# Norm closings in two parts of 256 tokens, in a two-block transformer forward pass

## The reference

```python
def _layer_norm(x, g, b):
    mu = jnp.mean(xf, -1, keepdims=True)
    var = jnp.mean(jnp.square(xf - mu), -1, keepdims=True)
    return (xf - mu) * lax.rsqrt(var + LN_EPS) * g + b

x = _layer_norm(ALPHA * x + h, ln1_g, ln1_b)             # twice a layer, 4 in all
x = _layer_norm(ALPHA * x + _sq_relu_mlp(x, w1, w2), ln2_g, ln2_b)
...
h = h + rms_norm(mix, ln_mix_post)                       # second block
a = rms_norm(h, ln_ffn_pre)
ff = (silu(a @ w_gate) * (a @ w_up)) @ w_down
h = h + rms_norm(ff, ln_ffn_post)
```

## Time and profile before

| | |
|---|---|
| median of 3 runs | 2173.42 us (2169.97 to 2177.93) |
| profiled execution | 2177.21 us, span 2175.4 us |
| granted PE clock, mean | 0.989 |
| PE busy | 2091.1 us, 96% |
| PEld busy | 1664.8 us, 77% |
| DVE busy | 1238.9 us, 57% |
| ACT busy | 812.7 us, 37% |
| POOL busy | 262.1 us, 12% |
| DMA | 179.24 MB, mean 82 GB/s |

### The profile page before, as it was taken

The page is one execution under the profiler, slowest core; times in us unless marked ns, Lnnn a source line. Parts: engine busy times, 40 slices in busy tenths (PEclk is TensorE's granted clock), DMA queues, the critical chain, the costliest instruction groups (busy, mean ns, idle before and its releaser), DMA issues. The chain is left out here.

```text
span 2175.4 us, 30851 instructions
## 1 busy us (share of the span) xinstructions
PE 2091.1 (96%) x12664; PEld 1664.8 (77%) x12664; DVE 1238.9 (57%) x1692; ACT 812.7 (37%) x1268; POOL 262.1 (12%) x266
## 2 busy tenths in 40 slices
PE   8999989999999999999999999999998899999996
PEld 6776867888888778888878888877666578888885
DVE  5547866642344576667563453467678638534544
ACT  4444234531332434444362322344224554222321
POOL 0000002000001000000201880020542010000002
PEclk9999999999999999999999999999999999999998
DMA  6120003222222122222122222223111042233221
GB/s 232 65 72 29 4 3 107 90 96 97 96 97 94 63 95 78 69 70 76 49 95 94 97 97 97 97 88 125 59 59 35 2 145 88 91 93 108 98 79 65
DMA packets 51676, 179.24 MB, mean 82 GB/s; under 512 B 5784, under 2 KB 5784, under 8 KB 51280
## 3 DMA queue, kind: packets, MB, share of 16 engines
q1 hardware_dynamic: 47712, 165.45, 22.9%
q10 hardware_dynamic: 3328, 8.13, 1.1%
q0 software_dynamic: 496, 3.69, 0.4%
HBM read 172.51 MB, written 4.21 MB: 81 GB/s over the span
## 5 line engine op out<-in xcount | busy, mean ns | idle before, releaser
L1150 DVE TENSOR_TENSOR w_lo<-w_raw,w_hi 128x1024 fp32r<-128x1024 f32 (+1 forms) x320 | 412.3, 1290 | 696.3 <-ACT w_hi L1143 696.0
L1248 PE MATMUL banks<-xh,w_hi 128*128 128x512 f32 x1560 | 624.6, 400 | 3.5 <-PEq L214 2.5
L1250 PE MATMUL banks<-xh,w_lo 128*128 128x512 f32 x1560 | 609.4, 391 | 0.0
L1249 PE MATMUL banks<-xl,w_hi 128*128 128x512 f32 x1560 | 609.3, 391 | 0.0
L1143 ACT ACTIVATE w_hi<-w_raw 128x1024 fp32r<-128x1024 f32 (+1 forms) x320 | 328.6, 1029 | 703.7 <-PE banks L1250 653.1
L1248 PEld LDWEIGHTS banks<-xh,w_hi 128*128 128x128 f32 x1560 | 294.1, 189 | 74.9 <-issue 13.3
L1250 PEld LDWEIGHTS banks<-xh,w_lo 128*128 128x128 f32 x1560 | 293.8, 188 | 62.8
L1249 PEld LDWEIGHTS banks<-xl,w_hi 128*128 128x128 f32 x1560 | 294.3, 189 | 58.6 <-issue 1.7
L1248 PE MATMUL banks<-hh,w_hi 128*128 128x512 f32 x688 | 269.8, 392 | 1.0 <-DVE hl L372 1.0
L1250 PE MATMUL banks<-hh,w_lo 128*128 128x512 f32 x688 | 267.7, 389 | 0.0
L1249 PE MATMUL banks<-hl,w_hi 128*128 128x512 f32 x688 | 267.7, 389 | 0.0
(11 more groups left out here) (513 smaller groups left out, 2558.2 us busy)
## 6 DMA issues: line engine op xcount, KB each, us to landing
w_raw<-in_w SPq DMA_DIRECT2D x128, 512.0 KB, 3.4
w_raw<-in_w_gu SPq DMA_DIRECT2D x44, 512.0 KB, 3.4
w_raw<-in_w_c_in SPq DMA_DIRECT2D x40, 512.0 KB, 3.4
w_raw<-in_w_ab_in SPq DMA_DIRECT2D x27, 512.0 KB, 3.5
w_raw<-in_w_in SPq DMA_DIRECT2D x25, 512.0 KB, 3.5
w_raw<-in_w_down SPq DMA_DIRECT2D x16, 384.0 KB, 3.1
w_raw<-in_w_down SPq DMA_DIRECT2D x16, 320.0 KB, 2.8
w_raw<-in_w_ab_out SPq DMA_DIRECT2D x8, 512.0 KB, 3.4
```

Source lines behind the costliest of these rows:

```text
L1150: dve.tensor_tensor(lo[:, 0:n], core.raw[u % RAW][:, 0:n], hi[:, 0:n].bitcast(F32), ALU.subtract).then_inc(core.split_ready, 1)
L1248: pe.matmul(bank, hi[:, w], src.xh[:, kk, :], start=kk == 0, stop=False)
L1249: pe.matmul(bank, hi[:, w], src.xl[:, kk, :], start=False, stop=False)
L1250: mm = pe.matmul(bank, lo[:, w], src.xh[:, kk, :], start=False, stop=last)
```

## The change

The 512 tokens are taken as two halves of 256 (HALVES) around each norm. In short:

- **Last block** (in_halves): the last block of a product with a norm has two PSUM banks. All tiles of its last unit are swept for the first half (256 columns), `half` is signalled, then for the second half. Between the tiles of the second sweep PE does the mean matmuls of the first half and begins those of the second (pe_half). If the block has two units, the first one's tiles are done half after half.
- **Closing** (act_last, dve_last, in place of act_tail, dve_tail): both engines do the first half's closing during the second sweep, then wait for unit_used and do the second half's.
- **Next product** (by_items, in place of outer behind a norm): tiles 0 to 2 are made and used as six half items, first half first, then tiles 3 to 7 whole. The mean matmuls that close the second half come after the first item (pe_second). The banks of three units are accumulated over column halves.
- **Squares and spill** of tiles 0 to 2 (norms 4, 5) wait until both halves are there.
- **Final norm**: tiles 0 to 4 in halves, 13 items; VectorE does all additions; stores go item by item, in turn from SP and ScalarE.
- The dummy matmuls behind norms are gone. A product with a norm takes one bank more, so the ring of banks turns one further.

The diff, cut to its core:

```diff
+HALVES = (slice(0, T // 2), slice(T // 2, T))
+IN_HALVES = 3
+FINAL_IN_HALVES = 5
+def in_items(n):
+    return [(k, cols) for cols in HALVES for k in range(n)] + [(k, slice(0, T)) for k in range(n, KD)]
 class LayerNorm:
-    def pe_tail(self, pe):
...
-        keep_busy(core, pe, SHIFT_BANK, 4)
+    def pe_half(self, pe, k):
+        if k == 0:
+            pe.wait_ge(s.pre, KD - 2)
+            pe.wait_ge(s.sum, KD - 2)
+            self.mean_begun(pe, 0)
+        if k == 1:
+            self.mean_done(pe, 0)
+            pe.wait_ge(s.ssum, KD - 2)
+            self.square_begun(pe, 0)
+            self.square_done(pe, 0)
+        if k == 3:
+            self.mean_begun(pe, 1)
+        if k == 4:
+            pe.wait_ge(s.var, 1)
+            self.square_begun(pe, 1)
+    def pe_second(self, pe):
+        self.mean_done(pe, 1)
+        self.square_done(pe, 1)
-    def act_tail(self, act):
+    def act_last(self, act, evac, whole):
+        square(0); mean_square(0); inverse(0); high(0); kept(0)
+        square(1); high(1); mean_square(1); kept(1); inverse(1); high(2); kept(2)
+        for i in range(IN_HALVES, 2 * IN_HALVES):
+            high(i); kept(i)
+        for i in range(2 * IN_HALVES, len(self.items)):
+            high(i); kept(i)
+            if i < 3 * IN_HALVES:
+                beside(2 * IN_HALVES - 1, i - 2 * IN_HALVES)
+            beside(i, i - IN_HALVES)
-    def dve_tail(self, dve):
+    def dve_last(self, dve, evac, whole):
+        dve.wait_ge(s.half, 1)
+        dve.wait_ge(s.pre, KD - 2)
+        block(0); var(0); less(0); less(1); less(2)
+        dve.wait_ge(s.inv, 2)
+        scale(0); scale(1)
+        whole()
+        block(1); scale(2); low(0); var(1); less(3); low(1); less(4); less(5)
+        dve.wait_ge(s.inv, 4)
+        scale(3); scale(4); low(2); scale(5); less(6); low(3); low(4); scale(6); low(5)
+        for i in range(7, len(self.items)):
+            less(i); low(i - 1); scale(i)
 class RmsPost:
-        if not self.late:
-            for k in range(1, KD, 2):
-                gp.wait_ge(s.normed, k + 1)
-                gp.tensor_tensor(core.X[:, k, :], core.X[:, k, :], core.Y[:, k, :], ALU.add).then_inc(s.x_pool, 1)
+    def pe_half(self, pe, k):
+        if k == 1:
+            pe.wait_ge(self.s.ssum, KD - 2)
+            self.square_begun(pe, 0)
+        if k == 2:
+            self.square_done(pe, 0)
+        if k == 4:
+            pe.wait_ge(self.s.inv, 1)
+            self.square_begun(pe, 1)
+    def dve_last(self, dve, evac, whole):
...
+        begun = 3 if self.late else 2
+        for i in range(begun):
+            norm(i)
+            if self.late and i:
+                low(i - 1)
+        whole()
+        if isinstance(evac, Accumulate):
+            block(1)
+        for i in range(begun, len(self.items)):
+            if self.items[i] == (0, HALVES[1]):
+                dve.wait_ge(s.inv, 4)
+            norm(i)
+            if self.late:
+                low(i - 1)
 class Chain:
+    def in_halves(self, pe, part, j, before):
+        def products(h, k):
+            pe.matmul(bank, hi[:, w], src.xh[:, kk, cols], start=kk == 0, stop=False)
+            pe.matmul(bank, hi[:, w], src.xl[:, kk, cols], start=False, stop=False)
+            return pe.matmul(bank, lo[:, w], src.xh[:, kk, cols], start=False, stop=last)
+        if i < part.U - 1:
+            for k in range(part.kts[i]):
+                for h in range(2):
+                    mm = products(h, k)
+        else:
+            for k in range(part.kts[i]):
+                mm = products(0, k)
+            mm.then_inc(part.norm.s.half, 1)
+            for k in range(part.kts[i]):
+                mm = products(1, k)
+                part.norm.pe_half(pe, k)
+        mm.then_inc(core.unit_used, 1)
+    def by_items(self, pe, part):
+        for n, (k, cols) in enumerate(src.items):
+            for i in units:
+                if i == 0:
+                    pe.wait_ge(src.src_hi, n + 1)
+                pe.matmul(banks[i][:, cols], hi[:, w], src.xh[:, k, cols], ...)
+                pe.matmul(banks[i][:, cols], lo[:, w], src.xh[:, k, cols], ...)
+            if n == 0:
+                src.pe_second(pe)
+            pe.wait_ge(src.src_lo, n + 1)
+            for i in units:
+                mm = pe.matmul(banks[i][:, cols], hi[:, w], src.xl[:, k, cols], ...)
```

More of the change, by code:

```diff
@@ new lines, in dve_last, with block, var, less @@
+    def dve_last(self, dve, evac, whole):
+        core, s, Y, line = self.core, self.s, self.core.Y, self.core.line
+        def block(h):
+            i, cols = self.b0 + KD - 1 + h, HALVES[h]
+            dve.tensor_tensor(Y[:, KD - 1, cols], Y[:, KD - 1, cols], core.bank(i)[:, cols], ALU.add).then_inc(core.freed(i), 1)
+        def var(h):
+            dve.wait_ge(s.kept, h + 1)
+            dve.wait_ge(s.e2, h + 1)
+            cols = HALVES[h]
+            dve.tensor_tensor(line[INV2][:, cols], core.psum[SQUARE_BANK][:, cols], line[INV2][:, cols], ALU.subtract).then_inc(s.var, 1)
+        def less(i):
+            k, cols = self.items[i]
+            y = self.tile(Y, k, cols)
+            dve.tensor_tensor(y, y, self.mean_of(k, cols), ALU.subtract).then_inc(s.less, 1)
+        def scale(i):
+            k, cols = self.items[i]
+            dve.wait_ge(s.less, i + 1)
+            dve.tensor_tensor(Y[:, k, cols], Y[:, k, cols], line[INV][:, cols], ALU.mult).then_inc(s.scaled, 1)
+        def low(i):
+            k, cols = self.items[i]
+            dve.wait_ge(s.src_hi, i + 1)
+            dve.wait_ge(s.x, i + 1)
+            hi = self.xh[:, k, cols].bitcast(F32)
@@ L931, in dve_tail @@
-        dve.tensor_tensor(line[INV2][:], core.psum[SQUARE_BANK], line[INV2][:], ALU.subtract).then_inc(s.var, 1)
+                dve.tensor_tensor(self.xl[:, k, cols], core.X[:, k, cols], hi, ALU.subtract).then_inc(s.src_lo, 1)
+        dve.wait_ge(s.half, 1)
+        dve.wait_ge(s.pre, KD - 2)
+        block(0)
+        var(0)
         less(0)
         less(1)
+        less(2)
         dve.wait_ge(s.inv, 2)
@@ L936, in dve_tail @@
         scale(1)
[L937 to L942, removed]
+        whole()
+        block(1)
+        scale(2)
+        low(0)
+        var(1)
+        less(3)
+        low(1)
+        less(4)
+        less(5)
+        dve.wait_ge(s.inv, 4)
+        scale(3)
+        scale(4)
+        low(2)
+        scale(5)
+        less(6)
+        low(3)
+        low(4)
+        scale(6)
+        low(5)
+        for i in range(7, len(self.items)):
+            less(i)
+            low(i - 1)
+            scale(i)
+        low(len(self.items) - 1)
 class RmsPost:
@@ L1163, in act @@
                 u = part.u0 + j
-                ends = part.norm and j == part.n - 1
+                if part.norm and j == part.n - 1:
+                    part.norm.act_last(act, part.of_block[-1][0], lambda: act.wait_ge(core.unit_used, u + 1))
+                    if u + SLOTS < self.splits:
+                        self.high(act, u + SLOTS)
+                    continue
                 act.wait_ge(core.unit_used, u + 1)
@@ L1176, in act @@
                         part.norm.act_block(act, b)
-                if ends:
-                    part.norm.act_tail(act)
                 if part.norm and u + SLOTS < self.splits:
@@ L1200, in dve @@
                 u = part.u0 + j
-                ends = part.norm and j == part.n - 1
+                if part.norm and j == part.n - 1:
+                    part.norm.dve_last(dve, part.of_block[-1][0], lambda: dve.wait_ge(core.unit_used, u + 1))
+                    if u + SLOTS < self.splits:
+                        self.low(dve, u + SLOTS)
+                    continue
                 dve.wait_ge(core.unit_used, u + 1)
@@ L1232, in pe @@
             src = part.source
-            if part.n_outer:
+            if part.n_outer and src.items:
+                self.by_items(pe, part)
+            elif part.n_outer:
                 self.outer(pe, part)
@@ L1241, in pe @@
                 before = sum(part.kts[:i])
+                if part.norm and b == KD - 1:
+                    self.in_halves(pe, part, j, before)
+                    continue
                 for k in range(part.kts[i]):
```

248 lines of the change are left out of this document (162 added, 86 removed).

## The result

The changed kernel is slower: 2183.58 us (median of 5) against 2173.13 (median of 5), ratio 1.004, 95% interval 1.0028 to 1.0052, that is 6 to 11 us more. The forecast was 2164.6, with 2160 to 2176 as its range. The profiled execution of after took 2183.58, its span is 2181.8, its mean granted clock 0.99.

A forecast was written before the change was run, and what follows sets the result against it. PE is busy 96% of the span, so time is won only where it waits or small steps run alone, around the six norms; -1.5 - 2.8 + 0.3 - 0.3 - 2.0 - 2.5 = -8.8 us from 2173.42 gives 2164.6, range 2160 to 2176.

The forecast's parts named there:

- Price (a): Product matmuls of 256 columns with a fresh 128x128 weight load: 0.12 us each, bounds 0.1125 and 0.131, or 0.19.
- B: Rival: halves cost more, matmuls at 0.131 or longer waits in the six half items; 2169.5 us, chance 0.25.
- D: Rival: 256-column matmuls at 0.1125 us each, 3.9 us better, 2160.7 us; chance 0.10.
- E: Rival: slower than before, weight load not hidden behind 256 columns; at 0.19 a matmul +28 us, 2193; chance 0.10.
- The first half's closing: Chain from the first half's add to the first xh: 4.73 us, covered almost exactly by PE's second half sweep.
- norm 1's stall: PE stalls 1.7 us before the closing mean matmul, since VectorE's add waits behind the weight split.
- Entry cost: Start of the next product behind norm 1: six half items take 8.85 us for what took 6.3, +2.55.
- Half items over 10 us: Next product's start: warning that the forecast is wrong above all if the half items take over 10 us.
- rival C: Half clock on PE after idle stretches in norm 3 adds 2.2 to 4.3 us, 2166.8 to 2168.9; chance 0.13.
- Norm 4: Like norm 1 on PE until item 6, then ScalarE's delayed squares give back about 1.2 us; net -0.3.
- Norm 2: Two weight units a block, VectorE free in time so no stall; -5.4 less 2.55, net -2.8 us.
- Norm 6: Kernel's end: first norm on VectorE at 2157.15 instead of 2160.44, last addition at 2170.4 instead of 2172.89; -2.5 us.

The follow-up runs named there:

- e1: Changed kernel with VectorE subtracting the low part two tiles back, not one, before each scaling of whole tiles in the layer norms' closing; 2171.64 us, ratio 0.9982 to before.
- e9: e4 plus two matmuls of 128x512 f32 that nobody reads, in TensorE's wait for GpSimd's sum in norm 3; 2164.83 us, ratio 0.9957.
- e4: e1 plus the layer norm's activation table load issued at the start of the closing, behind ScalarE's weight split; 2168.26 us, ratio 0.9971.
- e5: e4 plus VectorE adding the first half of the last block ahead of its weight split in the layer norms; 2159.88 us, ratio 0.994.

## Why the prediction was wrong

The sign was wrong, by a term that isn't in the sum. Step by step:

**Price (a), 256-column products at 0.12: right.** The first half sweep of after:

```profile
367.40 0.28 PE L1460 MATMUL banks<-xh,w_hi 128*128 128x256 f32 x1
...
370.51 0.28 PE L1462 MATMUL banks<-xh,w_lo 128*128 128x256 f32 x1
```

These are 27 matmuls, the 24 of the first half and three of the second: 26 spacings in 3.11 us, 0.12. By it B's and D's other prices (0.131, 0.1125) and E (0.19) fall.

**The first half's closing and norm 1's stall: right in kind.** In norm 1 the last sweep and the chain take 10.0 us together (367.40 to 377.41), as forecast (367.7 to 377.7). PE waits 1.4 instead of 1.7 in norm 1, not at all in norm 2, and twice in norm 3, 2.38 and 1.33 instead of 2.4 and 2.4:

```profile
1092.78 1.19 PE L863 MATMUL banks<-line,consts 128*128 128x256 f32 x2 [2.38 <-POOL line L937]
1095.94 1.22 PE L872 MATMUL banks<-Y,consts 128*128 128x256 f32 x2 [1.33 <-DVE Y L1003]
```

**Six half items in 8.85: right.** 377.41 to 386.36 in norm 1, 8.95.

**The failed step: what stands behind the half items.** Under "Entry cost" the sum lets the five whole tiles and the next sweep go on as before, 2.04 a tile. Their spacing is 2.95, and the next sweep starts 1.41 behind the last of them instead of 0.68. The diff showed it (`low(k - 2)` gone, `low(i - 1)` in); I counted its operations and not their order. Measured from start to start, scaling to xh 0.72, xh to X 0.72, X to low 0.90, low to the next scaling 0.61, it is 2.95; the rows of before gave nearly that, two VectorE operations of about 0.69 and two ScalarE ones of about 0.80, 3.0. PE's five whole tiles in norm 1 of after start 2.48, 2.95, 2.95 and 2.95 apart, the next sweep 2.92 behind the last of them, where each would be 2.04: +4.05, and e1 gave back 4.0 there. Over the four layer norms e1 gave back 13.7, and -8.8 + 13.7 = +4.9; the other 2.1 up to the measured +7.0 is norm 3's clock, with smaller differences in the other norms that cancel. It was no rival either. "Half items over 10 us" was the nearest of my warnings and looked at the wrong tiles.

**Norm 3: the mechanism of rival C, with a price of its own.** The clock fell (after: 0.54 and 0.61 where before has 1.00). I gave it 0.13 and 2.2 to 4.3 us; e9 measures 2.1 (up to 2.7, see there). With the clock at 1.00 norm 3 comes out at +0.05 in e9, near the forecast +0.3. It should have stood in the sum, since the sum itself held two new stalls of 2.4 there. The dummies' removal has no part in the fall: it comes during or just behind PE's first wait, inside the last sweep (after has 1.00 in 1090 to 1092 and 0.50 in 1092.4 to 1096), and the dummies stood behind that sweep.

```profile
1092.00:1096.00 4.00, 1.89 (x6) 0.54 0.30 112
1096.00:1100.00 4.00, 4.00 (x15) 0.61 0.40 131
```

The Trainium skill (TensorE: Matmul & The Clock Gate, "Part 1: The HAM clock gate") has an idle array throttled to half rate. The trace agrees in kind: after, e1 and e4 fell to 0.50 at or just behind the end of a wait of 2.38, 2.35 and 2.34 us, yet e5 stayed at 1.00 through one of 2.34, so that (C) was likely and not certain.

**Norm 4**: -0.3 predicted; without the ring -0.57 (e1). Its whole tiles are slower than PE's 2.04 there too (2.21, 2.11, 2.45 and 2.36 apart in e1), by ScalarE's squares and spills as expected, though less than the 2.65 counted, so it lost less to the ring (2.6) than norms 1 and 3. **Norm 2**: -2.8 against -2.27 without the ring; 0.4 of the difference is in its six half items, 9.22 in after (738.22 to 747.44) where 8.85 were counted. **Norm 5** (-2.0) measured -1.97. **Norm 6** (-2.5) measured -2.84. Its half tiles take 0.86 (0.87 planned; two of them start at 2168.20 and 2169.06), and the last addition is

```profile
2178.60 0.69 DVE L1185 TENSOR_TENSOR X<-X,Y 128x512 f32<-128x512 f32 x1
```

and the span ends 2.5 us after the last addition (2179.29 to 2181.8), as before.

Taken together: with the lag put back (e1) the six terms sum to -6.7 against -8.8 predicted. Norm 3 is 1.9 of that gap, about what its clock cost; that norms 2, 4 and 6, off by +0.5, -0.3 and -0.3, cancel is luck. Open stays what decides whether the clock falls behind such a wait, and what else than the clock scatters between the closings; the gap of e4's median to e1's beyond the closings (1.4 to 2.4 us) lies within that scatter.

## What to carry to other kernels

Where two in-order engines hand tiles to and fro, write down for each instruction what stands ahead of it in its queue, and add up every closed ring, not only the work of each engine: the pace of a tile is the longest ring, and the lag between producing and consuming decides how many tiles share one turn. When a change rewrites a loop, compare the order of its body with the old one before its costs. And price a closing on its own stretch of the trace, between two landmarks that both kernels have: here that resolves 0.15 us, where the intervals of the ratios are 4 to 9 us wide.

## What the runs showed of the hardware

- A VectorE subtraction of 128x1024 from two operands in SBUF takes 1.23 us alone and 2.14 to 2.25 beside a GpSimd addition or multiplication of 1.28 that started 0.12 to 0.23 earlier; where VectorE started 0.08 earlier, it took 1.23 and GpSimd 2.30 (before, 1587). Moving the subtraction earlier, into such a neighbour, gained 0.5 of 1.4 us (e4).
- PE's granted clock fell from 1.00 to 0.50 at or just behind the end of one wait of 2.34 to 2.38 us behind full work (after, e1, e4), stayed 1.00 through a wait of 2.34 (e5), and stayed 1.00 where two dummies lay in that wait (e9). One profiled execution each.
- 256-column float32r products with a fresh load each follow one another in 0.12 us, 512-column ones in 0.227: two halves cost 0.013 more than a whole.
